# Two transformer blocks on one core: projections and output projections in products of 512 columns, each weight load four depth tiles of a pair of column groups

## The reference

```python
hx = rmsnorm(x) * (1 + sc_a) + sh_a
ux = hx @ w_in[l]                     # 1024 x 2304
uc = hc @ (w_in[l] if ctx_out else w_in[l][:, OFF_K:OFF_HQ])
fx = fourier_mix(...); ax, ac = attention_group(...); rx, rc = hgrn_group(...)
x = x + g_a * (concatenate([fx, ax, rx], -1) @ w_out[l])      # 1024 x 1024
x = x + g_f * swiglu(rmsnorm(x) * (1 + sc_f) + sh_f, w_gate[l], w_up[l], w_down[l])
```

## Time and profile before

| | |
|---|---|
| median of 3 runs | 1890.02 us (1899.88, 1890.02, 1888.99) |
| profiled execution: first to last instruction | 1893.6 us |
| TensorE busy | 1752.4 us |
| VectorE, ScalarE busy | 1279.7 us, 837.7 us |
| HBM read | 296.52 MB |

### The profile page before, as it was taken

The page is one execution under the profiler, slowest core; times in us unless marked ns, Lnnn a source line. Parts: engine busy times, 40 slices in busy tenths (PEclk is TensorE's granted clock), DMA queues, the critical chain, the costliest instruction groups (busy, mean ns, idle before and its releaser), DMA issues. The chain is left out here.

```text
span 1893.6 us, 31178 instructions
## 1 busy us (share of the span) xinstructions
PE 1752.4 (93%) x12350; PEld 1575.5 (83%) x12350; DVE 1279.7 (68%) x2298; ACT 837.7 (44%) x1663; POOL 84.1 (4%) x154
## 2 busy tenths in 40 slices
PE   5899989899999999998788999988899998989998
PEld 3799867898888888898577999786899887879996
DVE  1335778558887666677775788868588885665554
ACT  2523764243222222345643444456543445665442
POOL 1000133000000000001030000000000000000000
PEclk9899999899999999999788999999999999999999
DMA  9442122056556655333334898642499874416653
GB/s 296 135 157 68 29 71 88 23 155 180 172 172 199 179 185 161 121 114 95 130 95 120 260 269 271 238 132 63 128 279 265 281 230 142 112 45 178 181 176 133
DMA packets 355184, 299.59 MB, mean 158 GB/s; under 512 B 8208, under 2 KB 325376, under 8 KB 354912
## 3 DMA queue, kind: packets, MB, share of 16 engines
q1 hardware_dynamic: 353616, 293.44, 50.9%
q0 software_dynamic: 1424, 4.16, 0.9%
HBM read 296.52 MB, written 1.05 MB: 157 GB/s over the span
## 5 line engine op out<-in xcount | busy, mean ns | idle before, releaser
L2293 DVE TENSOR_TENSOR wlow<-raw,whigh 128x2048 fp32r<-128x2048 f32 (+2 forms) x183 | 409.8, 2243 | 260.6 <-ACT whigh L1706 260.0
L1706 ACT ACTIVATE whigh<-raw 128x2048 fp32r<-128x2048 f32 (+2 forms) x183 | 343.1, 1878 | 302.0 <-PE bank L1035 93.1
L1035 PE MATMUL bank<-HTH,whigh 128*128 128x256 f32 (+1 forms) x1440 | 445.8, 310 | 6.2 <-issue 5.4
L1035 PE MATMUL bank<-HTH,wlow 128*128 128x256 f32 (+1 forms) x1440 | 442.2, 307 | 0.0
L1035 PE MATMUL bank<-HTL,whigh 128*128 128x256 f32 (+1 forms) x1440 | 442.1, 307 | 0.0
L1035 PE MATMUL bank<-whigh,HTH 128*128 128x256 f32 (+1 forms) x1008 | 295.5, 293 | 21.7 <-DVE HTL L2616 6.3
L1035 PEld LDWEIGHTS bank<-HTH,whigh 128*128 128x128 f32 x1440 | 275.7, 191 | 18.8 <-issue 5.8
L1035 PE MATMUL bank<-wlow,HTH 128*128 128x256 f32 (+1 forms) x1008 | 290.8, 288 | 0.0
L1035 PE MATMUL bank<-whigh,HTL 128*128 128x256 f32 (+1 forms) x1008 | 290.7, 288 | 0.0
L1035 PEld LDWEIGHTS bank<-HTH,wlow 128*128 128x128 f32 x1440 | 275.5, 191 | 12.6
L1035 PEld LDWEIGHTS bank<-HTL,whigh 128*128 128x128 f32 x1440 | 275.6, 191 | 11.7
(11 more groups left out here) (247 smaller groups left out, 2212.1 us busy)
## 6 DMA issues: line engine op xcount, KB each, us to landing
raw<-in_ffn_w_in SPq DMA_DIRECT2D x88, 512.0 KB, 5.4
A<-in_ada_w SPq DMA_DIRECT2D x38, 1024.0 KB, 7.2
A<-in_w_ada SPq DMA_DIRECT2D x28, 1024.0 KB, 5.5
raw<-in_w_gate SPq DMA_DIRECT2D x44, 512.0 KB, 5.4
raw<-in_w_up SPq DMA_DIRECT2D x44, 512.0 KB, 6.4
raw<-in_ffn_w_out SPq DMA_DIRECT2D x20, 1024.0 KB, 5.1
raw<-in_w_in SPq DMA_DIRECT2D x18, 1024.0 KB, 5.9
raw<-in_w_down SPq DMA_DIRECT2D x18, 1024.0 KB, 5.9
```

The source lines that it names most:

```text
L1035: return nc.tensor.matmul(out, lhsT, rhs, start=start, stop=stop, skip_group_check=True)
L1706: nc.scalar.activation(parts(loads[n])[0], raw_slot(loads[n]), ACT.Copy).then_inc(*made("split_high", loads[n]))
L2293: V.tensor_tensor(low, raw_slot(loads[n]), as_float(high), ALU.subtract).then_inc(*made("split_low", loads[n]))
```

## The change

Two neighbouring or chosen column groups make a pair (`win_pairs`). A load now holds four depth tiles of both groups of a pair: 4 x 512 in place of 8 x 256 elements. TensorE opens a bank for each token tile, adds depth tiles 0 to 3 with the first load and 4 to 7 with the second, 12 products of 512 columns each, and only the second load closes the banks. A group left over (`(8,)`, `(5,)`) goes as before. The output projections do the same with the two halves of 512 columns. In layer 1 the context has only one of the two groups in some pairs; those products keep 256 columns. The number of loads and their sizes stay.

With it move: the Fourier products, split in two steps over four tiles; the turned heads and the modulation of layer 0, which get banks 6 and 7 in layers 0 and 1 (`fixed`); VectorE's order in a load, where low parts of heads and Fourier copies come before the split; the context's norm turns in layer 1 (after x's second tile in both halves); the turn of the mix in the output projections.

```diff
+def win_pairs(l):
+    return ([(0, 3), (1, 2), (4, 5), (6, 7), (8,)], [(0, 3), (1, 2), (4, 5), (6, 7), (8,)], [(4, 5), (0, 1), (2, 3)],
+            [(6, 7), (8, 0), (2, 4), (1, 3), (5,)])[l]
...
+def project_steps(l):
     steps = []
+    for p, pair in enumerate(win_pairs(l)):
+        if (l, p) == (2, 0):
+            steps += [(p, half, t) for t in pair_tiles(l, p) for half in range(len(pair))]
+        else:
+            steps += [(p, half, t) for half in range(len(pair)) for t in pair_tiles(l, p)]
...
+def turns_after(l, p, half, t):
+    n = win_loads(l).index((p, half))
+    if l < 2:
+        return [("tile", n - 5)] if t == 1 and n >= 5 else []
+    if l == 2:
+        return {(2, 1): [("keys", 0), ("keys", 1)], (4, 1): [("queries", 0), ("queries", 1)]}.get((n, t), [])
+    return {(2, 1): [("keys", 0)], (3, 0): [("keys", 1)], (4, 1): [("queries", 0)], (6, 1): [("queries", 2)],
+            (7, 0): [("queries", 4)], (8, 1): [("queries", 1)]}.get((n, t), [])
+
+def fourier_after(l, p, half, t):
+    if l >= 2 or (p, half) != (1, 0):
+        return []
+    return [("columns", "rows")[t % 2], t // 2]
...
 def out_loads(l):
-    return [(8, 256)] * 4 if l < 3 else [(4, 512)] * 2
+    return ([(0, 0), (0, 4), (1, 0), (1, 4)], [(0, 0), (1, 0), (0, 4), (1, 4)], [(0, 0), (0, 4), (1, 0), (1, 4)], [(0, 0), (1, 0)])[l]
...
+            fixed = {"fa": lambda l, g, d: NBANKS + (g + d) % 2, "fy": lambda l, g: NBANKS + g, "ff": lambda l, g: NBANKS + g,
+                     "m": lambda l, t, b: NBANKS + t % 2}
+            heads_fixed = {"qT": lambda l, t: NBANKS, "kT": lambda l, t, b: NBANKS + 1}
...
(TensorE, project)
+                if l < 2:
+                    fixed.update(heads_fixed)
+                if l == 0:
+                    mod_bank.update({"sum": NBANKS, "mod": NBANKS + 1})
+                def some(p, half, t, ks):
...
+                    if ks[0] == 0:
+                        opened[t] = open_bank("u", l, p, t)
+                    r, c = tokens_of(l, t), slice(256 * cs[0], 256 * cs[-1] + 256)
+                    for k in ks:
+                        need_h(l, "mix", unit_of(l, "mix", t), k)
+                        n = k - depth[0]
+                        last = mm3(opened[t][:, c], (HTH[:, k, r], HTL[:, k, r]), (wh[:, n, c], wl[:, n, c]), k == 0, k == KD - 1)
+                    if ks[-1] == KD - 1:
+                        last.then_inc(*made("product", "u", l, p, t))
+                    elif ks[-1] == depth[-1] and ends_load(l, p, half, t):
+                        last.then_inc(*made("project_part", l, p))
...
+                    if (l, p, t) == (1, 0, 1):
+                        unit_turn(l, "mix", 1, range(2 * half, 2 * half + 2))
+                    if fourier_after(l, p, half, t):
+                        fourier(l, *fourier_after(l, p, half, t))
...
(TensorE, project_out)
+                for j, t in steps[:-1]:
+                    if (l, j, t) in ((0, 0, 0), (1, 2, 0)):
+                        mixed_turns(l, X_TILES)
+                    some(j, t)
...
(VectorE, project)
+                for at, (p, half) in enumerate(win_loads(l)):
+                    for t in pair_tiles(l, p):
+                        for turns in turns_after(l, p, half, t):
+                            heads_low(l, *turns)
+                        if fourier_after(l, p, half, t)[:1] == ["rows"]:
+                            fourier(l, fourier_after(l, p, half, t)[1])
+                    if ("win", l, p, half) != last_win(l):
+                        split(index["win", l, p, half] + HIGH)
```

More of the change, by code:

```diff
@@ L209, in late_queries, with ends_load, value_pair @@
+def ends_load(l, p, half, t):
+    return t == pair_tiles(l, p)[-1]
+def value_pair(l):
+    return pair_of(l, (3, 3, 5, 8)[l])
 def late_queries(layer):
-    return win_order(layer)[-2:] if layer >= 2 else ()
+    return ((), (), (2, 3), (3, 5))[layer]
 def queries_of(layer, p):
     return [p // 2] if layer == 2 else [(4 * g + p) // 2 for g in range(GROUPS3)]
[L219 to L232, removed]
+def turns_after(l, p, half, t):
[6 more added lines that the diff above has]
+            (7, 0): [("queries", 4)], (8, 1): [("queries", 1)]}.get((n, t), [])
@@ L260, in load_plan @@
     for l in range(4):
-        out += [("win", l, j) for j in win_order(l)]
+        out += [("win", l, *load) for load in win_loads(l)]
         out += [("wo", l, j) for j in range(len(out_loads(l)))]
@@ L866, in _ @@
                 if n >= RAW:
-                    if loads[used][0] == "win" and loads[used][2] == win_order(loads[used][1])[-1]:
+                    if loads[used] == last_win(loads[used][1]):
                         for spot, cs in ada_by.items():
@@ new lines, in project @@
+                opened, at_once = {}, l == 3
+                if l < 2:
[3 more added lines that the diff above has]
+                def some(p, half, t, ks):
+                    key = ("win", l, p, half)
+                    need_parts(key)
+                    depth, cs = win_depth(l, p, half), pair_columns(l, p, t)
+                    wh, wl = (w.rearrange("p (k c) -> p k c", k=len(depth)) for w in parts(key))
+                    if ks[0] == 0:
[9 more added lines that the diff above has]
+                        last.then_inc(*made("project_part", l, p))
@@ L1491, in project_out, with enter @@
             def project_out(l):
-                jobs, shape, entered, banks_of = out_jobs(l), out_loads(l), set(), {}
-                def enter(t):
-                    if t in entered:
+                steps, entered, banks_of = out_steps(l), set(), {}
+                if l == 0:
+                    fixed["x1"] = out_bank
+                def enter(t, k):
+                    if (t, k >= 6) in entered:
                         return
-                    entered.add(t)
+                    entered.add((t, k >= 6))
+                    if l < 2 and k >= 6:
+                        pe.wait_ge(*drained("m", l, t, 0))
+                        return
                     for t2 in X_TILES if l == 3 else (t,):
```

356 lines of the change are left out of this document (168 added, 188 removed).

## The result

The changed kernel takes 1880.4 us, the median of ten runs (1875.3 to 1887.5); the kernel before takes 1894.6 us beside it (1889.0 to 1904.9). The ratio is 0.992, with a 95% interval of 0.990 to 0.994: 14 to 15 us gained where 31 were forecast, and 1880 us lie above the range of 1849 to 1877. The two profiled spans are 1893.6 and 1879.0 us, 14.6 us apart.

A forecast was written before the change was run, and what follows sets the result against it. TensorE, busy 93% of the span, was taken as the bound nearly everywhere. Stage terms 18.4 + 3.4 + 0.4 - 2.0 + 4.3 + 0.75 + 5.5 = 30.8 us, off the 1890.0 us median, gave 1859, stated as 1860; range 1849 to 1877.

The forecast's parts named there:

- The products: Projections and output projections: 1344 pairs of 256-column products become 512-column ones, each saving 0.013 us, 17.5 us in all.
- Layer 0, projection: Layer 0's input projection: waits of 5.29 and 3.41 us and their low clock go, products shorten; 18.4 us gained.
- Layer 1, projection: Layer 1's input projection: 3.1 us of products gained, mostly lost to uncovered norm turns and a split; 0.4 us gained.
- Gone is one wait: Layer 1's projection: a 1.5 us wait for a ring bank at 860.7 goes; end at 882.2 instead of 882.6.
- Layer 1, output: Layer 1's output projection: a new 4.6 us wait for load three's low split; 2.0 us lost, bounds 0 and 4.
- Layer 2, projection: Layer 2's input projection: the 2.06 us wait of the keys' turn is covered; 4.3 us gained, bounds 2 and 6.
- a whole half load: Layer 2's projection: 5.4 us now lie between the keys' closing and their turn, which had waited 2.06 us.
- Layer 3, projection: Layer 3's input projection: 2.5 us of products, and waits of 2.20 and 2.67 us go; 5.5 us gained net.
- Rival (a): Whole kernel: the waits only move, only the products' 17.5 us stay, about 1873 us; chance 0.20.
- (b): Products: the width pays only 0.003 us a pair, products give 4 and waits 13, about 1873 us; chance 0.03.
- (c): Weight loads: low splits end after TensorE's arrival, 2.29 us per paying load; 1914 us if 24 pay; chance 0.05.
- (d): Whole kernel: more comes free than counted, layer 1's waits are hidden and tails shrink, 1850 us; chance 0.07.

The follow-up runs named there:

- e1: Changed kernel with its order kept, but the 512-column products issued as two groups of 256 columns: median 1889.4 us, ratio 0.998 to the kernel before.
- e8: The changed kernel itself, unaltered, run and profiled once more: ratio 0.992 to the kernel before.
- e7: Changed kernel with layer 1's Fourier products after its fourth load instead of its third: ratio 0.992 to the kernel before.
- e11: Changed kernel with layer 3's input projection reading adjacent tokens instead of every second one: that projection takes 56.7 us against 57.7.
- e3: Changed kernel with layer 1's x before context tiles, its third output load split before the mix, keys copied before the split in layers 2 and 3: ratio 0.986.
- e4: Kernel before, with 256-column products and only layer 0's projection order and banks from the change: ratio 0.993, some 12.5 us less.
- e6: e3 with layer 1's Fourier part also one load later: ratio 0.986 to the kernel before.
- e10: e3 with layer 1's Fourier columns behind the third load's second tile and rows behind the fourth load's first tile: ratio 0.983 to the kernel before.
- e9: Changed kernel with layer 1's input projection in single column groups, plus e3's output-split and key-copy orders: 1864.8 us, ratio 0.983 to the kernel before.

## Why the prediction was half right

The direction, the bound and most places were right. The forecast gave 0.74 to a gain of 1% or more; 0.8% came. The size was off by 16 us: -14.6 by the spans in place of -30.8.

- The products: 13 ns a pair stands (0.120 and 0.227 us in the rows of both kernels), but 17.5 us was too much; e1 gives about 10. Layer 3 accounts for 1.3 of the difference (the stride: 1.2 us came instead of 2.5). In layer 1's projection the busy time gives 2.1 for 3.1. Some of the rest is time that TensorE spends in waits once its products are shorter (e1: 2.5 us in layer 1's projection).
- Layer 0, projection: -17.1 of -18.4; both waits and most of the low clock went. Output: -3.4 of -3.4.
- Layer 1, projection: the step that failed, +5.65 in place of -0.4. The norm's uncovered turns and the split behind them were sized well (1.85, 1.85, 0.98 for 1.75, 1.75, 1.1). What failed is "Gone is one wait ... Following it load by load, the projection ends at 882.2": the forecast had the second turn of the norm at 811.0, 7.4 us later than before, and did not move GpSimd's loads along with it, which are issued behind its last low piece. With the 4.3 us that such a load had taken, that alone would have cost a few tenths; it took 6.0, and the wait was 1.95 us (7.4 and 3.3 us in e8). Then 1.8 us of low clock came into the projection; a wait of 0.75 us was left at the first turned heads; the width gave 1.0 less; and the first wait was 0.3 longer. That is 5.8 of the 6.05. The low clock is not the Fourier wait's alone: e7 has as much of it without that wait, and two more profiles of these same instructions have 6.8 and 10.2 us in this stage (e8 and e11, 101.5 and 100.4 us).
- Layer 1, output: +3.1 for +2.0. The new wait is 4.65 us for 4.6, and its stretch of low clock (1014.7 to 1018.2) came as counted; what is over lies in the low clock at the start of the stage, until 1001.1.
- Layer 2, projection: -2.4 for -4.3. That "a whole half load" lies between the keys' closing and their turn was true of TensorE, but on VectorE a split stood ahead of the copies, and e3's reorder brought 1.7. Output: -0.9 for -0.75, but e8 has +0.7 there, with 3 us more of low clock.
- Layer 3, projection: -3.6 for -5.5 with one stretch of low clock, -5.1 without (e8).
- Other stages: +4.1 for 0. The forecast put them at nothing because the change does not touch them. Layer 0's first gate and up products (+0.5) and layer 1's down products (+0.7 or more) did grow with it; for the rest it is not shown.
- Rival (a), that the waits only move, is refuted for layer 0 by e4. For layer 1 it describes what happened to the pairs: e7, e6 and e10 each removed a wait and met a smaller or another one. (b) is out by the rows, and its time of 1873 was missed too. (c) did not occur: TensorE waits for a low split at two places in the seven stages, 0.98 and 4.65 us. (d) did not occur either: with layer 1's waits hidden, e9 and e10 come to 0.983, which is the size of the forecast (0.984) and not (d)'s 0.979.

What stays open: why the down weights land late and the low clock differs by several us from run to run, and why GpSimd's loads take longer with pairs in layer 1. No run isolated these.

## What to carry to other kernels

When work is moved in one engine's order, list everything that hangs on it, the loads that other engines issue behind it included, and by what margin each was met; a margin (5.3 us here) doesn't show in the waits of the trace before. Wider products are worth their fixed part only where TensorE is the bound: in layer 1's projection waits for ScalarE and VectorE took what the width saved (91.3 us with the best order of the pairs, 91.2 without pairs), and the reordering that the pairs forced cost 7.7 us. And cut both profiles by stage before a difference is explained, then take a second profile of the same code: here one stage moved by 7 us with nothing changed.

## What the runs showed of the hardware

- A stretch of 3.4 us at half the clock (1.2 in place of 2.4 GHz) costs 1.5 us where TensorE is busy throughout: 128.28 against 126.78 us. The fourteen profiles have 106 to 147 us of it altogether. The wait and low clock that the change took from layer 0's projection did not lower the sum (124 and 110 us in the two profiles before, 127 and 127 after).
- An operand loaded into TensorE with a stride of two elements slows 512-column products from 0.227 to 0.234 us on average (e11); at 256 columns layer 3 had 0.120 as all others.
- The same small load by GpSimd's queue (`in_hg_norm`, layer 1) landed 4.3 to 4.4 us after its issue in the five profiles where the next weight load was issued 4.0 us behind it, and 5.9 to 7.8 us in the nine where that was at most 1.9 us.
